# A conformer, latent-attention and mixture-of-experts trunk: two depthwise blocks move to TensorE

## The reference, cut to what matters

```python
def conformer_conv_module(h, norm_g, pw1_w, pw1_b, dw_w, dw_b, ln_g, ln_b, pw2_w, pw2_b):
    hn = rms_norm(h, norm_g)
    a, gate = jnp.split(hn @ pw1_w + pw1_b, 2, axis=-1)
    u = a * jax.nn.sigmoid(gate)
    u = lax.conv_general_dilated(
        u, dw_w[:, None, :].astype(u.dtype), window_strides=(1,),
        padding=[(CONV_WIDTH - 1, 0)],
        dimension_numbers=('NWC', 'WIO', 'NWC'),
        feature_group_count=D_MODEL) + dw_b
    u = jax.nn.silu(layer_norm(u, ln_g, ln_b))
    return u @ pw2_w + pw2_b

def reference(x, ...):
    cos, sin = rope_tables(positions)
    h = x
    for layer in range(DEPTH):                      # DEPTH = 2
        if layer < N_A_LAYERS:                      # layer 0
            h = h + conformer_conv_module(h, ...)
        else:                                       # layer 1
            k_shared, v_shared = shared_mla_kv(h, ..., cos, sin)
            h = h + mla_attention_layer(h, k_shared, v_shared, ..., cos, sin)
        h = h + hierarchical_moe(h, ...)            # 32 experts, top 2 within the best of 4 groups
    return h
```

## Time and profile before

| | us |
|---|---|
| median of 3 runs | 1105.11 (1104.97 to 1106.36) |
| the profiled execution | 1109.35 |
| its span in the profile | 1107.6 |

### The profile page before, as it was taken

One profiled execution on the slowest core, in us unless ns is written; L12 is line 12 of the kernel. 1 busy time (PEld: TensorE's weight loads), 2 busy tenths in 40 slices (PEclk: granted clock), 3 DMA queues, 4 the chain that ended last, 5 costly groups with the idle time before them and its releaser, 6 DMA issues.

```text
span 1107.6 us, 11501 instructions
## 1 busy us (share of the span) xinstructions
PE 996.1 (90%) x4840; PEld 433.4 (39%) x4840; DVE 240.3 (22%) x534; ACT 175.9 (16%) x449; POOL 58.4 (5%) x92
## 2 busy tenths in 40 slices
PE   8999999989797979889799999998988989897886
PEld 7885533232232323223255664332323232232321
DVE  6993420101020100101026624201010101010101
ACT  3876120000000000000044523000000000000000
POOL 2890000000000000000000000000000000000000
PEclk8999999999999999999999999999998999999999
DMA  9786899999999999999996659999999999999996
GB/s 313 219 350 261 317 424 425 427 430 427 427 428 429 427 427 427 429 428 427 398 380 242 266 217 368 430 428 427 428 427 429 426 430 426 427 425 431 428 420 260
DMA packets 67311, 430.73 MB, mean 389 GB/s; under 512 B 12358, under 2 KB 22685, under 8 KB 46524
## 3 DMA queue, kind: packets, MB, share of 16 engines
q1 hardware_dynamic: 67134, 429.86, 94.5%
q10 hardware_dynamic: 126, 0.14, 0.0%
HBM read 428.94 MB, written 1.05 MB: 388 GB/s over the span
## 4 chain that ended last, share of the span: by engine, by line
PE 47%; DMA 45%; SPq 4%; ACT 1%; DVE 1%; issue 1%; POOL 0%; ACTq 0%; DVEq 0%
DMA ring<-in_w_down_dram 30%; DMA zone<-in_w_down_dram 15%; PE bank L1019 11%; PE bank L1075 8%; PE bank L1124 6%; PE bank L904 5%; SPq L477 3%; PE bank L1328 3%; PE bank L947 3%; PE bank L1084 2%; PE bank L1215 1%; PE bank L1008 1%; PE bank L1237 1%; PE bank L1191 1%; PE bank L1199 1%
## 5 line engine op out<-in xcount | busy, mean ns | idle before, releaser
L1019 PE MATMUL bank<-ring,zone 128*32 128x512 f32 x1136 | 326.7, 611 | 39.9 <-DMA ring<-in_w_gate_up_dram 27.2
L1019 PE MATMUL bank<-zone 128*32 128x512 f32 x872 | 261.9, 605 | 30.3 <-DMA ring<-in_w_gate_up_dram 16.7
L1019 PEld LDWEIGHTS bank<-ring,zone 128*32 128x32 f32 x1136 | 86.0, 112 | 214.1 <-issue 213.9
L1075 PE MATMUL bank<-ring,xT 128*32 128x512 f32 x496 | 142.8, 601 | 11.3 <-DMA ring<-in_w_down_dram 6.7
L1019 PEld LDWEIGHTS bank<-zone 128*32 128x32 f32 x872 | 67.3, 111 | 146.7 <-issue 146.7
L1569 DVE TENSOR_TENSOR xT<-xT,bank 128x512 f32<-128x512 f32 x14 | 9.6, 688 | 444.0 <-PE bank L1019 444.0
L1574 DVE TENSOR_TENSOR h<-bank,h 128x512 f32<-128x512 f32 x64 | 44.3, 692 | 261.5 <-PE bank L1124 261.3
L1075 PE MATMUL bank<-zone,xT 128*32 128x512 f32 x272 | 91.6, 593 | 4.9 <-DMA ring<-in_w_down_dram 2.0
L745 ACT ACTIVATE xT<-bank 128x512 f32<-128x512 f32 x14 | 8.4, 597 | 505.4 <-PE bank L1019 505.4
L1075 PEld LDWEIGHTS bank<-ring,xT 128*32 128x32 f32 x496 | 37.9, 111 | 83.5 <-issue 78.2
L1124 PE MATMUL bank<-zone,xT 128*128 128x512 f32 x128 | 63.4, 616 | 0.4
(11 more groups left out here) (280 smaller groups left out, 689.6 us busy)
## 6 DMA issues: line engine op xcount, KB each, us to landing
ring<-in_w_gate_up_dram SPq DMA_DIRECT2D x70, 2048.0 KB, 36.8
zone<-in_w_gate_up_dram SPq DMA_DIRECT2D x54, 2048.0 KB, 34.6
ring<-in_w_down_dram SPq DMA_DIRECT2D x38, 2048.0 KB, 36.1
zone<-in_w_down_dram SPq DMA_DIRECT2D x20, 2048.0 KB, 37.3
ring<-in_w_down_dram SPq DMA_DIRECT2D x12, 1024.0 KB, 15.4
ring<-in_a_pw_w_dram SPq DMA_DIRECT2D x8, 1024.0 KB, 12.1
ring<-in_a_pw_w_dram SPq DMA_DIRECT2D x2, 2048.0 KB, 11.5
ring<-in_w_o_dram SPq DMA_DIRECT2D x2, 2048.0 KB, 20.9
```

The costliest lines, as they stand in the source:

```text
L1019: ins = nc.tensor.matmul(bank[b][s * CAP:(s + 1) * CAP, :], xs[:, k, s * CAP:(s + 1) * CAP], rhs[s][:, b * HALF:(b + 1) * HALF], start=(k ...
L1075: ins = nc.tensor.matmul(bank[2 + b][s * CAP:(s + 1) * CAP, :], hidT[:, k, s * CAP:(s + 1) * CAP], units[s][:, k, b * HALF:(b + 1) * HALF] ...
```

## The change

Blocks 5 and 6 are now convolved on TensorE in another form. For block i and each group q of 32 channels, `u4[i]` holds on partitions 32j to 32j+31 the same 32 channels shifted by 8j columns, j = 0 to 3; ScalarE makes it by 16 copies of 32 partitions by 263 columns (`shifted`). A matmul then contracts four taps at once: its weights `bands[:, i, q, step, :]` (128 x 32) hold, at partition 32j+c and column c, the tap 8j+step of channel 32q+c. Eight steps (step = 0 to 7) make 32 taps, the last with weight zero; the four groups q write four quarters of the partitions of one bank. The weights come from a small table `tap_sets` (VectorE, 16 copies of 32 partitions), a folded identity `eye4` (VectorE, one reduction) and two multiplications of 1024 columns on GpSimd.

Blocks 0, 2, 4 stay whole on VectorE, block 1 on GpSimd; block 3 is shared with 14 taps on VectorE and 17 on GpSimd, block 7 with 19 and 12. The 31 diagonals are gone. The means of seven blocks are issued ahead for both halves t, and block 7's two matmuls close them. The copy to `cols` moves from `n == 3` to `n == 4`. GpSimd makes `mean_w` and the bands ahead of adding the bias to `h`, and SyncE issues the bias row after the fourth piece of the first projection's weights. The tap table, in the diff's new form, and the changed loops:

```diff
-        u_sb = spot(0, KD, PAD + S)
+        u_sb = spot(0, KD, PAD + S + 1)
...
-        diag = spot(2 * UNIT, CW, P)
+        ON_DVE, ON_POOL, ON_PE, SHARED = (0, 2, 4), 1, (5, 6), {3: 14, 7: 19}
+        SHIFTS, STEPS, PART = 4, 8, P // 4
+        WIDE = S + STEPS - 1
+        bands = spot(2 * UNIT, 2 * SHIFTS * STEPS, PART).rearrange("p (i q s) c -> p i q s c", q=SHIFTS, s=STEPS)
+        tap_sets = spot(3904, 2 * SHIFTS, STEPS).rearrange("p (i q) s -> p i q s", q=SHIFTS)
+        eye4 = spot(3904 + 2 * SHIFTS * STEPS, PART)
...
+        u4 = [xn_flat[:, P + 2 * S:P + 2 * S + SHIFTS * WIDE].rearrange("p (q x) -> p q x", q=SHIFTS), spot(at_u4, SHIFTS, WIDE)]
...
-        side = [xn[:, 1, i * S:(i + 1) * S] for i in range(4)]
-        ON_DVE, ON_POOL, ON_PE, SHARED, SPLIT = (0, 2, 3, 5), (1, 4), 6, 7, 16
+        side = [xn_flat[:, P + i * S:P + (i + 1) * S] for i in range(2)]
+        side += [spot(at_u4 + SHIFTS * WIDE + i * S, S) for i in range(3)]
...
-        SUMS = [(ON_POOL[0], cv[:, ON_POOL[0], :], side[0], 0), (ON_POOL[1], cv[:, ON_POOL[1], :], side[1], 0), (SHARED, side[2], side[3], SPLIT)]
+        SUMS = [(ON_POOL, cv[:, ON_POOL, :], side[0], 0), (3, side[1], side[2], SHARED[3]), (7, side[3], side[4], SHARED[7])]
...
-            sp.dma_start(pw2_b_row, a["a_pw2_b"].to_broadcast([P, D])).then_inc(small_in, 16)
...
+                if i == 4:
+                    sp.dma_start(pw2_b_row, a["a_pw2_b"].to_broadcast([P, D])).then_inc(small_in, 16)
                 pw1_in(i)
...
             nc.gpsimd.memset(u_sb[:, :, 0:PAD], 0.0).then_inc(set_by_pool, 1)
+            pool.wait_ge(tr_done, 4)
+            nc.gpsimd.memset(mean_w, 1.0 / D).then_inc(set_by_pool, 1)
+            pool.wait_ge(dw_ready, 2)
+            for i in range(2):
+                nc.gpsimd.tensor_tensor(bands[:, i, :, :, :], eye4.unsqueeze(1).unsqueeze(1).to_broadcast([P, SHIFTS, STEPS, PART]),
+                                        tap_sets[:, i, :, :].unsqueeze(3).to_broadcast([P, SHIFTS, STEPS, PART]),
+                                        ALU.mult).then_inc(bands_ready, 1)
             pool.wait_ge(small_in, 16)
             pool.wait_ge(xn_ready, 2)
             for t in range(TT):
                 nc.gpsimd.tensor_tensor(h[:, t, :], h[:, t, :], pw2_b_row, ALU.add).then_inc(hb_ready, 1)
-
-            pool.wait_ge(tr_done, 4)
-            nc.gpsimd.memset(mean_w, 1.0 / D).then_inc(set_by_pool, 1)
 
...
-            made, diags = iter(range(sum(CW - w0 for _, _, _, w0 in SUMS))), iter(range(CW))
+            made = iter(range(sum(CW - w0 for _, _, _, w0 in SUMS)))
...
+            def some_products(n):
+
+                for _ in range(n):
+                    if (p := next(made, None)) is not None:
+                        product(p)
+
+            def shifted(i):
+
+                act.wait_ge(u_ready, ON_PE[i] + 1)
+                for q in range(SHIFTS):
+                    for j in range(SHIFTS):
+                        ins = nc.scalar.copy(u4[i][j * PART:(j + 1) * PART, q, :], u_sb[q * PART:(q + 1) * PART, ON_PE[i], STEPS * j:STEPS * j + WIDE])
+                    ins.then_inc(u4_ready, 1)
+
...
-                for _ in range((0, 10, 10, 10, 10, 10, 10, CW)[m]):
-                    if (p := next(made, None)) is not None:
-                        product(p)
-                for _ in range((8, 0, 6, 6, 6, 6, 0, 0)[m]):
-                    if (i := next(diags, None)) is not None:
-                        nc.scalar.activation(diag[:, i, :], ident[:, :], ACT.Copy, scale=dwT[:, ON_PE, i:i + 1]).then_inc(diag_ready, 1)
-            act.wait_ge(pe_conv_done, 1)
-            nc.scalar.activation(cv[:, ON_PE, :], bank[2][:, 0:S], ACT.Identity, bias=col("dw_b", ON_PE)).then_inc(conv_act, 1)
+                some_products((0, 12, 9, 10, 15, 2, 0, CW)[m])
+                if m in ON_PE:
+                    shifted(ON_PE.index(m))
+            for i, m in enumerate(ON_PE):
+                act.wait_ge(pe_conv_done, i + 1)
+                nc.scalar.activation(cv[:, m, :], bank[4 + i][:, 0:S], ACT.Identity, bias=col("dw_b", m)).then_inc(conv_act, 1)
...
-            pe.wait_ge(u_ready, ON_PE + 1)
-            for w in range(CW):
-                pe.wait_ge(diag_ready, w + 1)
-                ins = nc.tensor.matmul(bank[2][:, 0:S], diag[:, w, :], u_sb[:, ON_PE, w:w + S], start=(w == 0), stop=(w == CW - 1))
-            ins.then_inc(pe_conv_done, 1)
+            for i in range(2):
+                pe.wait_ge(bands_ready, i + 1)
+                pe.wait_ge(u4_ready, SHIFTS * (i + 1))
+                for step in range(STEPS):
+                    for q in range(SHIFTS):
+                        ins = nc.tensor.matmul(bank[4 + i][q * PART:(q + 1) * PART, 0:S], bands[:, i, q, step, :], u4[i][:, q, step:step + S],
+                                               start=(step == 0), stop=(step == STEPS - 1))
+                ins.then_inc(pe_conv_done, 1)
             pe.wait_ge(cols_ready, 2)
             pe.wait_ge(set_by_pool, 2)
-            order = ON_DVE[0:3] + ON_POOL + ON_DVE[3:] + (ON_PE, SHARED)
-            for t in range(TT):
-                for i, m in enumerate(order):
-                    if t == 0:
-                        if m in ON_DVE:
-                            pe.wait_ge(conv_dve, ON_DVE.index(m) + 1)
-                        elif m in ON_POOL:
-                            pe.wait_ge(pool_added, sums_done(ON_POOL.index(m)))
-                        elif m == ON_PE:
-                            pe.wait_ge(conv_act, 1)
-                        else:
-                            pe.wait_ge(conv_dve, len(ON_DVE) + 1)
-                    ins = nc.tensor.matmul(bank[3 - t][:, 0:P], mean_w, cv[:, m, t * P:(t + 1) * P],
-                                           start=(i == 0), stop=(i == KD - 1))
-                ins.then_inc(mean_done, 1)
+            for last in (False, True):
+                for t in range(TT):
+                    for m in (7,) if last else (0, 2, ON_POOL, 4, 3) + ON_PE:
+                        if t == 0:
+                            if m in ON_DVE:
+                                pe.wait_ge(conv_dve, ON_DVE.index(m) + 1)
+                            elif m == ON_POOL:
+                                pe.wait_ge(pool_added, sums_done(0))
+                            elif m in ON_PE:
+                                pe.wait_ge(conv_act, ON_PE.index(m) + 1)
+                            else:
+                                pe.wait_ge(conv_dve, 5 if last else 4)
+                        ins = nc.tensor.matmul(bank[3 - t][:, 0:P], mean_w, cv[:, m, t * P:(t + 1) * P], start=(m == 0), stop=last)
+                    if last:
+                        ins.then_inc(mean_done, 1)
...
+            dve.wait_ge(set_by_pool, 1)
+            V.tensor_reduce(eye4, ident[:, :].rearrange("p (j c) -> p c j", j=SHIFTS), AX_X, ALU.add)
+            for j in range(SHIFTS):
+                n = min(STEPS, CW - STEPS * j)
+                for q in range(SHIFTS):
+                    ins = V.tensor_copy(tap_sets[j * PART:(j + 1) * PART, :, q, 0:n],
+                                        dwT[q * PART:(q + 1) * PART, ON_PE[0]:ON_PE[1] + 1, STEPS * j:STEPS * j + n])
+            ins.then_inc(dw_ready, 1)
...
-            for n, m in enumerate(ON_DVE + (SHARED,)):
-                width = CW if m != SHARED else SPLIT
+            for n, m in enumerate(ON_DVE + tuple(SHARED)):
+                width = SHARED.get(m, CW)
...
-                if m == SHARED:
+                if m in SHARED:
                     V.tensor_tensor(cv[:, m, :], cv[:, m, :], chain[1], ALU.add).then_inc(tap_done, 1)
                     taps += 1
                     dve.wait_ge(tap_done, taps)
-                    dve.wait_ge(pool_added, sums_done(2))
-                    V.tensor_tensor(cv[:, m, :], cv[:, m, :], side[2], ALU.add).then_inc(conv_dve, 1)
+                    b = 1 + tuple(SHARED).index(m)
+                    dve.wait_ge(pool_added, sums_done(b))
+                    V.tensor_tensor(cv[:, m, :], cv[:, m, :], SUMS[b][1], ALU.add).then_inc(conv_dve, 1)
                 else:
                     V.tensor_tensor(cv[:, m, :], cv[:, m, :], chain[1], ALU.add).then_inc(conv_dve, 1)
-                if n == 3:
+                if n == 4:
                     dve.wait_ge(cols_tr, 3)
                     V.tensor_copy(cols[:, N_EARLY:N_ROWS], bank[3][:, 0:N_ROWS - N_EARLY]).then_inc(cols_ready, 1)
```

22 lines of the change are left out of this document (14 added, 8 removed).

## The result

The change made the kernel slower: 1110.58 us (median of 6 runs, 1109.23 to 1114.9) against 1105.09 (6 runs, 1104.6 to 1107.41), a ratio of 1.0046 with a 95% interval of 1.0034 to 1.0058, or 3.8 to 6.4 us. The profiled execution took 1110.49, with a span of 1108.8.

A forecast was written before the change was run, and what follows sets the result against it. A chain of waits up to the second projection at 90.99 us, then mostly DMA, was taken as the bound; -0.2 (chain) + 1.5 (clock) = +1.3 us gave 1106.4 from 1105.11, range 1103.8 to 1108.7.

The forecast's parts named there:

- The last block closes 3.44 us earlier: VectorE's last addition, closing block 7, was to end at 80.60 us instead of 84.04.
- the distance of the copies: ScalarE's copies of 32 partitions by 263 columns were to start 0.31 us apart and stay hidden, with 0.1 to spare.
- the second rival: Copies on ScalarE cost 0.41 us each, delaying the last sigmoid and GpSimd's sum by 1.9: 1108.3 us; chance 0.13.
- Two convolutions at 3.5 us: On TensorE, blocks 5 and 6 were to take 3.5 us each, four matmuls running side by side.
- the fifth rival: TensorE's four matmuls overlap badly or weight loading bounds them; block 6 ends at 83.1, total 1107.2 us; chance 0.05.
- The copy to cols holds all means: The late-column copy, now behind VectorE's fifth block, makes all 16 TensorE means wait until 80.8 us.
- From the last addition to the projection: Means, subtractions and variance up to the second projection: 0.2 us won overall at full clock, plus 1.5 lost to the clock.
- The idle clock at 1.5: TensorE's 4.7 us pause before the means was to lower its clock, costing 1.5 us between 0 and 3.3.
- The first rival: TensorE's pause does not lower the clock, or only inside itself: 1104.9 us; chance 0.13.
- The early edits cost nothing: VectorE's reduction and 16 tiny copies, GpSimd's bands and the later residual bias cost nothing unless the angles end late.
- the third rival: VectorE's angles collide with GpSimd's residual additions, held up to 2.3 us; about 1.2 come out: 1107.6 us; chance 0.06.
- One to one to the end: A microsecond won or lost before the second projection at 90.99 us moves the end by as much.

The follow-up runs named there:

- e4: Changed kernel with 4 copies a group over all 128 partitions instead of 16 of 32, shifts between quarters left out: ratio 1.0021 to the original kernel.
- e11: Changed kernel with one more wait: GpSimd's band multiplications and residual additions wait for the end of the angles; ratio 1.0042 to the original kernel.
- e1: Changed kernel with the copy of the late columns back behind VectorE's fourth block: ratio 1.0013 to the original kernel, median 1107.58 us.
- e3: Original kernel with its copy of the late columns moved behind VectorE's fifth, last block: ratio 1.0024 to the original kernel.
- e2: Changed kernel with 14 unused 256-column matmuls on TensorE behind the convolution, filling its pause: ratio 1.0033 to the original kernel.
- e7: e1 with unused matmuls where TensorE would be idle (convolution, closing means, variance): ratio 1.0008 to the original kernel, median 1106.95 us.
- e8: e7 with e4's 4 copies a group instead of 16, so two blocks are not the reference's: ratio 0.9990 to the original kernel, 1104.32 us.
- e9: Original kernel with 30 of the 31 matmuls of block 6's convolution left out, so TensorE idles: ratio 1.0019 to the original kernel.
- e12: e7 plus GpSimd waiting for the angles and 4 of block 6's 16 copies moved to VectorE: ratio 0.9988 to the original kernel, 1105.16 us.
- e6: e1 with 8 of the 16 copies for block 6 made by VectorE instead of ScalarE: ratio 1.0012 to the original kernel.

## Why the prediction was wrong

The forecast was +1.3 us, no change to be told; measured were +5.1 (3.8 to 6.4), slower, and above the range.

- **The last block closes 3.44 us earlier: wrong, and this is the step that failed.** Within one kind of execution it closes 0.68 (early) or 0.86 (late) earlier. The term that was mis-sized is the distance of the copies, taken at 0.31 and measured at 0.42, 32 times; this was the second rival, priced at +1.9 (with it the forecast would have been 1108.3, still 2.3 too low). In the late kind, on which the sum was worked out, they cost 2.5: e4, without the narrow copies, closes the last block at 80.70, forecast 80.60, and e11 at 83.18. In the early execution of the kernel after an estimate from its rows gives 2.3: 0.31 apart, the first group lets sigmoid 6 go at 60.8, GLU 6 is stored when VectorE comes to it (62.9), the second group lets the last sigmoid go at 68.05 instead of 70.31, and the last addition follows that by 11.46, as it did, at 79.5. The other 0.5 of the 3.44 is the kind of execution: from 82.45 to 79.5 it is 2.9.
- **Two convolutions at 3.5 us: right**, 3.68 and 3.65; the fifth rival is out.
- **The copy to cols holds all means: right.** The first mean starts 0.06 behind it, and e1 and e3 move the time by 3.6 and 2.6.
- **From the last addition to the projection: right in the sum, partly by luck.** Forecast were 10.19 at full clock (80.60 to 90.79, which is 90.99 less 0.2) and 1.5 for the clock, 11.69; measured are 11.81 (81.77 to 93.58). Three sizes in it were off and offset each other. From the last addition to the first subtraction 4.3 us were forecast; e2, at full clock, has 3.85. Behind that something was left out: before, the variance of the first half was under way when the second subtraction came, and the projection followed that by 4.59; now the two subtractions come together, the second one starts 1.28 behind the first, at 88.62, and the projection 4.96 behind that. The clock is the third.
- **The idle clock at 1.5: borne out by the rows**, 1.72 between e2 and the kernel after, though the pause was 7.75 long and not 4.7. The time says 1.4, with overlapping intervals. The first rival is out: the clock stayed low for 3.6 us of the means.
- **The early edits cost nothing: partly wrong.** What the third rival describes is there in e7 and e8, 2.23 for an operation of 0.20. What it adds on average was not settled; in the profiled execution of after it did not occur, and its first GLU was 0.5 earlier than in e9.
- **One to one to the end: right**, by the 14 rows of the table. But the forecast set a shift worked out on an execution 4.24 above the median onto the median, as if the same engine were the last one there.

The forecast's 1.3, the 2.76 by which the last block closes later than forecast (3.44 less 0.68) and 0.12 from there to the projection are 4.2, inside the measured interval of 3.8 to 6.4; the 0.9 to the 5.1 stays open. The 2.76 are 2.3 of copies and 0.5 of the kind of execution; this split is worked out, not measured. That e8, with the late columns, the pause and the narrow copies taken away, is 6.2 us below the kernel after, where the prices of the single edits (3.6 + 1.4 + 2.8) give 7.8, fits the 2.3 that its unused matmuls cost in the profiled execution, but the intervals are too wide to show it.

## What to carry to other kernels

Before a shift is taken from a profile, look what kind of execution it shows, and compare like with like: here a first sigmoid 2 us late, as in 6 of 14 profiled executions, had made another engine the last one, and a gain of 2.27 read across the kinds is 0.7 to 0.9 within them. When work leaves an engine that a later stage needs, ask whether its clock stays up, and price the pause (here 7.75 us of waiting came with 6.8 us at a granted clock of 0.50); filling it can cost as much as it saves where the filling stands ahead of the real work (1.8 us in e12 and 2.3 in e8, against 1.7 saved in e2). A copy whose price is unknown is priced at both ends times its count: 32 copies with 0.11 us of doubt are 3.5 us, and 2.3 to 3.4 of them came out at the last block.

## What was not expected of the hardware

- ScalarE's COPY of 263 columns, SBUF to SBUF, lasts 0.41 us at 32, 64 and 128 partitions; the next starts after 0.31 at 128 and after 0.42 to 0.43 at 32 and 64. On VectorE the same copy of 32 partitions lasts 0.29, and four took 1.21 (e12).
- GpSimd's multiplication of 1024 columns with two broadcast inputs took 1.9 us (two in 3.78, after), its addition of as many plain ones 2.3 (two in 4.66).
- The low clock behind a pause came and lasted differently from one execution to the next: 3.4 us in e1 (the longest wait before it 1.99) and e4 (4.70), 6.8 in after (7.75), e6 (1.95) and e11 (7.06); and in e3, behind 2.87 of waiting, it did not come.
